# One plain step fewer in each up map of a two-layer trunk in three-pass fp32, with the low parts shared out anew

## The reference, cut to what matters

```python
D_MODEL = 1024; SEQ = 512; DEPTH = 2
D_FF = 2816            # ((8 * D_MODEL // 3 + 127) // 128) * 128

def conv_ffn(h, w_up, w_dw, b_dw, w_down):
    up = jnp.einsum("bsd,df->bsf", h, w_up)
    act, gate = up[..., :D_FF], up[..., D_FF:]
    act = causal_dwconv(act, w_dw, b_dw)          # width 3, along the sequence
    return jnp.einsum("bsf,fd->bsd", jax.nn.silu(act) * gate, w_down)

def reference(x, ...):
    for i in range(DEPTH):
        h = rmsnorm(x, norm_mix[i])
        x = x + conformer_conv_module(h, ...)      # layer 0; layer 1: multiscale_pool_mixer
        h = rmsnorm(x, norm_ffn[i])
        x = x + conv_ffn(h, ffn_w_up[i], ffn_w_dw[i], ffn_b_dw[i], ffn_w_down[i])
    return rmsnorm(x, final_norm)
```

## Time and profile before

| | us |
|---|---|
| median of 3 runs (lowest to highest) | 918.83 (917.87 to 919.42) |
| the profiled execution's own time | 919.51 |
| its span, first to last instruction | 917.7 |
| PE busy | 905.4 |
| DVE busy | 677.4 |
| ACT busy | 451.0 |
| POOL busy | 128.6 |

### The profile page before, as it was taken

One profiled execution on the slowest core, in us unless ns is written; L12 is line 12 of the kernel. 1 busy time (PEld: TensorE's weight loads), 2 busy tenths in 40 slices (PEclk: granted clock), 3 DMA queues, 4 the chain that ended last, 5 costly groups with the idle time before them and its releaser, 6 DMA issues.

```text
span 917.7 us, 14955 instructions
## 1 busy us (share of the span) xinstructions
PE 905.4 (99%) x6036; PEld 808.2 (88%) x6036; DVE 677.4 (74%) x827; ACT 451.0 (49%) x659; POOL 128.6 (14%) x102
## 2 busy tenths in 40 slices
PE   8999999999999999999999999999999999999997
PEld 7888888888889999998888898888999999888887
DVE  6999986569879999888343459898799999833333
ACT  7663557345435565565222455553455566532330
POOL 0475844000000000036000020000000001700000
PEclk9999999999999999999999999999999999999999
DMA  7323030332232233313323241233222231332212
GB/s 255 127 92 113 11 111 1 98 132 92 70 92 93 92 114 118 115 54 105 115 75 124 102 151 47 92 114 92 93 92 93 92 121 41 130 123 95 94 64 92
DMA packets 48160, 90.14 MB, mean 98 GB/s; under 512 B 3424, under 2 KB 35424, under 8 KB 44640
## 3 DMA queue, kind: packets, MB, share of 16 engines
q1 hardware_dynamic: 47520, 88.72, 28.8%
q10 hardware_dynamic: 576, 0.52, 0.2%
HBM read 86.09 MB, written 2.10 MB: 96 GB/s over the span
## 4 chain that ended last, share of the span: by engine, by line
PE 79%; DVE 6%; DMA 4%; issue 3%; POOL 3%; ACT 2%; SPq 1%; DVEq 0%; ACTq 0%
PE bank L1623 17%; PE bank L1625 17%; PE bank L1624 17%; PE bank L1924 5%; PE bank L1929 5%; PE bank L1925 5%; DMA raw_both<-w_up 3%; POOL u_lo L515 2%; PE bank L1665 1%; ACT pair_hi L907 1%; DVE bank L1303 1%; DVE pair_sum L1411 1%; DVE pair_sum L1413 1%; DVE pair_lo L1425 1%; DVE pair_sum L1407 1%
## 5 line engine op out<-in xcount | busy, mean ns | idle before, releaser
L1101 DVE TENSOR_TENSOR w_lo<-w_raw,w_hi 128x1408 fp32r<-128x1408 f32 (+2 forms) x51 | 94.8, 1858 | 66.8 <-ACT w_hi L639 66.1
L639 ACT ACTIVATE w_hi<-w_raw 128x1408 fp32r<-128x1408 f32 (+2 forms) x57 | 91.1, 1598 | 97.0 <-PE bank L1625 96.1
L1624 PE MATMUL bank<-u_lo,w_hi 128*128 128x512 f32 (+1 forms) x330 | 123.7, 375 | 0.0
L1924 PE MATMUL bank<-mixed,pair_hi 128*128 128x256 f32 x448 | 112.6, 284 | 0.5 <-DVE act_in L1431 0.3
L1925 PE MATMUL bank<-mixed,pair_hi 128*128 128x256 f32 x448 | 112.3, 283 | 0.0
L515 POOL TENSOR_TENSOR u_lo<-u_sum,late_hi 128x512 fp32r<-128x512 f32 x24 | 41.6, 1772 | 485.4 <-ACT late_hi L958 485.4
L907 ACT ACTIVATE pair_hi<-pair_sum 128x1024 fp32r<-128x1024 f32 x56 | 59.4, 1061 | 80.3 <-DVE pair_sum L1404 33.8
L1623 PE MATMUL bank<-f_hi,w_hi 128*128 128x512 f32 x240 | 94.0, 392 | 0.0
L1625 PE MATMUL bank<-f_hi,w_lo 128*128 128x512 f32 x240 | 93.4, 389 | 0.0
L1624 PE MATMUL bank<-f_lo,w_hi 128*128 128x512 f32 x240 | 93.4, 389 | 0.0
L1623 PE MATMUL bank<-late_hi,w_hi 128*128 128x512 f32 (+1 forms) x240 | 90.1, 376 | 0.0
(11 more groups left out here) (291 smaller groups left out, 2086.9 us busy)
## 6 DMA issues: line engine op xcount, KB each, us to landing
...
raw_both<-w_up SPq DMA_DIRECT2D x28, 512.0 KB, 4.1
...
raw_corner<-w_up SPq DMA_DIRECT2D x28, 256.0 KB, 3.8
raw_both<-w_up SPq DMA_DIRECT2D x28, 256.0 KB, 3.1
x_res<-x SPq DMA_DIRECT2D x3, 512.0 KB, 7.8
...
```

The source lines that it names most:

```text
L639: nc.scalar.activation(w_hi[s][:, 0:columns], w_raw[s][:, 0:columns], ACT.Copy).then_inc(w_rounded[s], 1)
L1101: V.tensor_tensor(w_lo[s][:, 0:columns], w_raw[s][:, 0:columns], as_f32(w_hi[s][:, 0:columns]), SUB).then_inc(w_split[s], 1)
L1624: M.matmul(dst, a, lo, start=False, stop=False)
L1924: M.matmul(dst, weights, hi[:, k, :], start=which in (1, 5) and k == 0, stop=False, skip_group_check=True)
```

## The change

Four things are changed, in both layers.

- `PLAIN` is 3. Each up map has 3 plain and 8 fast steps. `add_mixed` for all four mixed operands moves ahead of the gate in step 1, `split_as_is` of 0 behind the gate of step 1 and of 1 into step 2. In the first fast step PE takes, for the act tiles, high x high, then low x high, then high x low, and waits for the token operand's low part only ahead of the last. The gate's product and the low part of `u` of the last plain step are made inside the first fast step (`use_plain`, `round_u`, `split_u`).
- The low parts of the mixed operands of products 7 and 4 are made by POOL (`split_mixed` in its program), with a semaphore of their own.
- POOL makes 10 late low parts instead of 12; DVE makes those of late chunks 6 and 7 too.
- `add_corner` stands ahead of the split of the next step's product 1 on DVE, and on SP the corner's DMAs stand behind the near ones of their step, instead of ahead of them.

```diff
-PLAIN = 4
+PLAIN = 3
-LATE_GROUPS = {6: 4, 10: 8, 14: 12}
-END_GROUPS = {18: 2, 20: 4}
-END = 4
+LATE_GROUPS = {6: 4, 10: 6, 14: 10}
+END_CHUNKS = (6, 7, 12, 13, 14, 15)
+END_GROUPS = {12: 2, 18: 4, 20: 6}
+END = len(END_CHUNKS)
...
+            def split_mixed(layer, product):
+                n = MIXED[product]
+                pool.wait_ge(mixed_rounded, 4 * layer + n + 1)
+                pool.wait_ge(mixed_added, 4 * (layer + 1))
+                nc.gpsimd.tensor_tensor(mixed[n][:, 1, :, :], mixed_whole[n][:, :, :], as_f32(mixed[n][:, 0, :, :]), SUB).then_inc(last_mixed_split, 1)
...
-            for c in range(LATE - END):
-                split_late(0, c)
+            split_mixed(0, 7)
+            split_mixed(0, 4)
+            for c in range(LATE):
+                if c not in END_CHUNKS:
+                    split_late(0, c)
...
             def silu(layer, i, t):
+                if i == PLAIN:
+                    act.wait_ge(u_split[t], EARLY // 2 * (layer + 1))
...
                 copy_second(layer, i)
+                if i == PLAIN:
+                    for t in range(2):
+                        round_u(layer, i - 1, t)
...
                 if i == 1:
-                    add_mixed(layer, 5)
-                    add_mixed(layer, 6)
-                if i == 2:
-                    split_as_is(layer, 0)
+                    for product in (5, 6, 7, 4):
+                        add_mixed(layer, product)
+                if i == PLAIN - 1:
+                    split_as_is(layer, 1)
...
                 if i == 1:
-                    add_mixed(layer, 7)
-                    add_mixed(layer, 4)
                     split_mixed(layer, 5)
                     split_mixed(layer, 6)
-                if i == 2:
-                    split_as_is(layer, 1)
-                    split_mixed(layer, 7)
-                    split_mixed(layer, 4)
+                    split_as_is(layer, 0)
...
                 if i > PLAIN:
                     use_gate(layer, i - 1, 0)
                     use_gate(layer, i - 1, 1)
+                else:
+                    use_plain(layer, i - 1, 0)
+                    use_plain(layer, i - 1, 1)
                 split_pair(layer, i, 7)
                 split_pair(layer, i, 2)
                 if not last:
                     split_pair(layer, i, 4)
-                    split_pair(layer, i + 1, 1)
                 add_corner(layer, i)
                 if last:
                     split_pair(layer, i, 4)
-                if not last:
+                else:
+                    split_pair(layer, i + 1, 1)
                     add_pair(layer, i + 1, 5)
                 add_gate_corner(layer, i)
                 add_edge(layer, i)
                 if last:
+                    split_end(layer, 6)
+                    split_end(layer, 7)
                     split_down(layer)
                 conv_rest(layer, i, 0)
                 add_gate_edge(layer, i)
+                if i == PLAIN:
+                    split_u(layer, i - 1, 0)
+                    split_u(layer, i - 1, 1)
...
                 for k in range(KH):
-                    weights = pair_hi[slot][:, tiles, k, :]
-                    M.matmul(dst, weights, hi[:, k, :], start=which in (1, 5) and k == 0, stop=False, skip_group_check=True)
-                    M.matmul(dst, weights, lo[:, k, :], start=False, stop=False, skip_group_check=True)
+                    M.matmul(dst, weights[k], hi[:, k, :], start=which in (1, 5) and k == 0, stop=False, skip_group_check=True)
+                    if not early:
+                        M.matmul(dst, weights[k], lo[:, k, :], start=False, stop=False, skip_group_check=True)
...
+                if early:
+                    if which in MIXED:
+                        if which in (7, 4):
+                            pe.wait_ge(last_mixed_split, 2 * layer + MIXED[which] - 1)
+                        else:
+                            pe.wait_ge(mixed_split, 2 * layer + MIXED[which] + 1)
+                    else:
+                        pe.wait_ge(as_is_split, 2 * layer + (1 if which == 1 else 2))
+                    for k in range(KH):
+                        last = M.matmul(dst, weights[k], lo[:, k, :], start=False, stop=which in (2, 3, 4) and k == KH - 1, skip_group_check=True)
```

More of the change, by code:

```diff
@@ L626, in _ @@
             nc.gpsimd.tensor_tensor(band_first[:, :, 0:START], as_f32(plain[:, :, P:P + START]), as_f32(starts), ADD).then_inc(first_rounded, 1)
-            for c in range(LATE - END):
-                split_late(1, c)
+            split_mixed(1, 7)
+            split_mixed(1, 4)
+            for c in range(LATE):
+                if c not in END_CHUNKS:
+                    split_late(1, c)
         CONSTS = 10 + 2 * PHASES + max(WINDOWS) - 1
@@ L864, in plain_step @@
                     round_unit(1, m + i + 1, UNIT)
-                if i < EARLY // 2:
+                if i < PLAIN - 1:
                     for t in range(2):
-                        act.wait_ge(drained[2 + t], f + i + 1)
-                        nc.scalar.activation(u_hi[:, 2 * i + t, :], y[:, t, :], ACT.Copy).then_inc(u_rounded[t], 1)
+                        round_u(layer, i, t)
                 if i == 0:
@@ L874, in plain_step, with round_u @@
                     round_mixed(layer, 4)
+            def round_u(layer, i, t):
+                act.wait_ge(drained[2 + t], DRAINED_UP[layer] + i + 1)
+                nc.scalar.activation(u_hi[:, 2 * i + t, :], y[:, t, :], ACT.Copy).then_inc(u_rounded[t], 1)
             def round_mixed(layer, product):
@@ L1920, in product @@
                     hi, lo = [as_is[at][:, tokens, part, :, :] for part in range(2)]
+                weights = [pair_hi[slot][:, tiles, k, :] for k in range(KH)]
+                early = i == PLAIN and tiles == ACT_TILES
                 for k in range(KH):
-                    weights = pair_hi[slot][:, tiles, k, :]
-                    M.matmul(dst, weights, hi[:, k, :], start=which in (1, 5) and k == 0, stop=False, skip_group_check=True)
-                    M.matmul(dst, weights, lo[:, k, :], start=False, stop=False, skip_group_check=True)
+                    M.matmul(dst, weights[k], hi[:, k, :], start=which in (1, 5) and k == 0, stop=False, skip_group_check=True)
+                    if not early:
+                        M.matmul(dst, weights[k], lo[:, k, :], start=False, stop=False, skip_group_check=True)
                 if tiles == ACT_TILES:
@@ L1928, in product @@
                 for k in range(KH):
-                    last = M.matmul(dst, pair_lo[slot][:, tiles, k, :], hi[:, k, :], start=False, stop=which in (2, 3, 4) and k == KH - 1, skip_group_check=True)
+                    last = M.matmul(dst, pair_lo[slot][:, tiles, k, :], hi[:, k, :], start=False, stop=which in (2, 3, 4) and k == KH - 1 and not early, skip_group_check=True)
+                if early:
[8 more added lines that the diff above has]
+                        last = M.matmul(dst, weights[k], lo[:, k, :], start=False, stop=which in (2, 3, 4) and k == KH - 1, skip_group_check=True)
                 last.then_inc(act_done if tiles == ACT_TILES else pair_done, 1)
```

44 lines of the change are left out of this document (25 added, 19 removed).

## The result

| kernel | median us | lowest to highest | executions | ratio, 95% interval |
|---|---|---|---|---|
| before | 919.12 | 917.87 to 919.67 | 4 | |
| after | 934.44 | 934.02 to 934.82 | 4 | 1.0163 [1.0149, 1.0177] |

The change makes the kernel 15.3 us slower. The prediction said 921.9 and a range up to 924.0: the sign is right, the size is not.

What follows compares the result with a forecast made beforehand. PE, busy 99%, was taken to bound the kernel. From the profiled 919.5 us: - 3.2 - 1.1 - 0.6 + 0.3 + 7.7 gave 922.6, as a median 921.9; range 914.2 to 924.0.

Steps and rivals of the forecast that it cites:

- The steps: PE, up maps: one plain step of 21.76 us becomes a fast one of 20.15 per layer, 3.2 us less in all.
- The operands on POOL: First fast steps: POOL's subtractions hold DVE, `act_in` is 4.6 us late, PE pauses 3.1 and 4.6 us, 7.7 together.
- Hidden: Rival: POOL's low parts don't hold DVE, so the kernel is not slower, 914.3 us; chance 0.20.
- half price: Rival: DVE is only 2 to 3 us late from POOL, pauses 1 + 2.5, time 918 us; chance 0.16.
- the third rival: Fast steps: the corner's DMA, queued behind near, lands late, +3.5 us, 925.4; chance 0.10, shared with a higher POOL price.
- PE waits in every fast step: Named sign, in the changed profile's fast steps, that the prediction is wrong; no size given.
- The corner pauses: Fast steps, product 4: PE's three pauses for the corner's sum go, 1.06 us less.
- The late low parts: End of the up maps: PE's two waits for POOL's late low parts go, 0.6 us less.
- Second fast step: Product 3's low part comes late behind two u low parts on DVE: +0.3 us for both layers (0 to 1.0).

Runs made afterwards that it cites:

- a_sp: Kernel after, with SP's DMA order put back as before (corner ahead of the near pair): 923.74 us.
- b_corner: Kernel before, with only the corner's sum on DVE moved ahead of the split of the next near product: 917.70 us.
- a_sp_low: Kernel after, with SP's old DMA order and the low parts of mixed operands 7 and 4 both made by DVE: 918.49 us.
- a_sp_one: Kernel after, with SP's old DMA order; DVE makes the low part of mixed operand 7, POOL that of 4: 921.50 us.
- a_sp_keep: Kernel after, with SP's old DMA order and extra unread matmuls filling PE's pauses in the first fast steps: 923.22 us.
- b_sp: Kernel before, with only SP's DMA order changed (near pair ahead of the corner): 928.18 us.
- b_late: Kernel before, with only the low parts of late chunks 6 and 7 moved from POOL to DVE: 918.23 us.
- c_fast: Kernel after, with SP's old DMA order; DVE makes the low parts of mixed operands 7 and 4 inside the first fast step: 917.67 us.

## Why the prediction was wrong

- **The steps, -3.2.** Right: 20.15 to 20.18 us for an undisturbed fast step in a_sp and b_corner.
- **The operands on POOL, +7.7.** Right in mechanism and size. A subtraction of 1024 columns takes 2.41 us (estimate 2.4); `act_in` is 4.4 us late by POOL (4.6), and the pauses are 2.8 and 4.3 us (3.1 and 4.6). a_sp_low and a_sp_one show it by dose. Less DVE's own 2.27, the pauses of a_sp_low come to nothing in layer 0 and 0.2 in layer 1, where the working had 0.1 for a POOL that costs nothing. Two of its sums are slightly off and change nothing: by its own rows layer 1's pause is 3.1 + 32.4 - 30.7 = 4.8 and not 4.6, and the upper bound 7.7 + 8.8 = 16.5. "Hidden" and "half price" fall: POOL got in between DVE's instructions at once, both times.
- **The clock behind the pauses, no term.** 1.6 + 2.6 = 4.2 us of matmuls at the lower level in the kernel after. The sum priced a pause by its own length. a_sp_keep shows the price on the spot (1.5 us in layer 0), not in the kernel's time.
- **The corner's transfer behind the near pair: the step that failed.** The sum had no term for it; the third rival gave it 3.5 us, and a chance of 0.10 together with a higher price of POOL. It asked when the corner would land and took the near pair's 4.1 us as given. The near pair itself is what comes late, by 1.1 us, and it stands in a loop that has no room for it. The trace of before showed the loop: issued at 300.69, in ACT's hands at 305.55 (4.86 us), at DVE 1.09 later, and 14.23 us to the next issue at 320.87. That is 20.18 us, no less than PE's 20.15, and DVE waits for ACT ahead of the split of product 1, 0.24 us in this step and 5.5 in the 14 together:

```profile
300.69 0.81 SPq L492 DMA_DIRECT2D raw_both<-w_up  x2
320.87 0.82 SPq L492 DMA_DIRECT2D raw_both<-w_up  x2
```
```profile
305.55 1.06 ACT L907 ACTIVATE pair_hi<-raw_both 128x1024 fp32r<-128x1024 f32 x1 [1.02 <-DMA raw_both<-w_up]
```
```profile
306.64 1.23 DVE L1425 TENSOR_TENSOR pair_lo<-raw_both,pair_hi 128x1024 fp32r<-128x1024 f32 x1 [0.24 <-ACT pair_hi L907]
```

  For the size: b_sp puts the cost at 9.0 us, a_sp at 9.6, the stretches of after at 10.4. The prediction named "PE waits in every fast step" as a sign that it is wrong, but didn't work out when that would be. The sign came: from the third fast step on, every step of the kernel after takes 20.7 to 21.4 us from start to start.
- **The corner pauses, -1.1.** Right in sign, and the size fits: the stretches of before held 0.9 and 0.7 us above seven undisturbed steps, and b_corner gains 0.8 (0.1 to 1.7).
- **The late low parts, -0.6.** Not found: b_late shows no difference. PE's waits for POOL go, but at the next unit of the down map PE then waits 0.4 to 0.5 us for DVE's `w_lo`: in b_late and c_fast in layer 1, in a_sp_low in both.
- **Second fast step, +0.3.** 0.1 in either layer in a_sp (20.26 and 20.27 from start to start of PE); in c_fast, where DVE has more to do there, 1.2 and 1.6.

The forecast for the profiled execution was 922.6. With 4.2 for the clock and 10.4 for the loop it is 937.2; less 0.5 for the pauses, 0.6 since before held more pauses in its stretches than the 1.1 of the sum, 0.3 for the second step and 1.0 for the part outside the stretches, beyond the 0.6 forecast, it is 934.8, as measured. The 10.4 is what was left of the stretches, so this sum closes by the way it is made; what bears it out are the 9.6 of a_sp and the 9.0 of b_sp.
